# First mixer of a two-block transformer in fp32: gates and output projections with tokens on the partitions, and an earlier start condition for the differential heads

## What is computed

```python
h = rmsnorm(x, norm_mix_g)
u = h @ w_in                                   # 1024 x 5376
u_rwkv, u_attn, u_gate = split(u, [1792, 3328])
o_a = rwkv7_time_mix(u_rwkv, ...)              # 256 x 512
o_b = diff_attention(u_attn, ...)              # 256 x 512, 4 heads
g_a, g_b = split(sigmoid(u_gate), 2)           # 256 x 1024 each
merged = g_a * (o_a @ w_proj_a) + g_b * (o_b @ w_proj_b)
x = x + merged @ w_out
h = rmsnorm(x, norm_mlp_g)                     # and on to w_ff1, w_ff2, ...
```

## Time and profile before

| | us |
|---|---|
| median of 3 runs | 1442.97 (1442.38 to 1443.07) |
| time of the profiled execution | 1442.83 |
| span of the profiled execution | 1441.0 |
| TensorE busy (matmuls) | 1431.8 |
| VectorE busy | 1015.3 |
| ScalarE busy | 766.0 |

### The profile page before, as it was taken

One profiled execution on the slowest core, in us unless ns is written; L12 is line 12 of the kernel. 1 busy time (PEld: TensorE's weight loads), 2 busy tenths in 40 slices (PEclk: granted clock), 3 DMA queues, 4 the chain that ended last, 5 costly groups with the idle time before them and its releaser, 6 DMA issues.

```text
span 1441.0 us, 22851 instructions
## 1 busy us (share of the span) xinstructions
PE 1431.8 (99%) x9408; PEld 1233.0 (86%) x9408; DVE 1015.3 (70%) x1347; ACT 766.0 (53%) x1038; POOL 26.3 (2%) x93
## 2 busy tenths in 40 slices
PE   9999999999999999999999999999999999999999
PEld 8988898888888888888878888888888877788887
DVE  6866577886457887558768786478774688688753
ACT  7744474655336555445766555355553556665532
POOL 0000000000001100000000000000000000000000
PEclk9999999999999999999999999999999999999999
DMA  8431225555554555545424555545555453255552
GB/s 335 172 121 62 89 102 220 197 204 189 191 175 176 205 186 194 194 157 205 147 90 174 198 183 201 183 171 205 178 202 185 160 181 135 91 204 186 194 188 86
DMA packets 36103, 249.11 MB, mean 173 GB/s; under 512 B 4128, under 2 KB 4256, under 8 KB 6688
## 3 DMA queue, kind: packets, MB, share of 16 engines
q1 hardware_dynamic: 35712, 247.46, 48.3%
q10 hardware_dynamic: 288, 0.19, 0.1%
HBM read 246.59 MB, written 1.05 MB: 172 GB/s over the span
## 4 chain that ended last, share of the span: by engine, by line
PE 97%; DMA 1%; ACT 1%; DVE 1%; issue 0%; SPq 0%; DVEq 0%; ACTq 0%
PE ps L2007 24%; PE ps L1922 16%; PE ps L1924 16%; PE ps L1923 16%; PE ps L2014 12%; PE ps L1997 2%; PE ps L2143 1%; PE ps L1996 1%; DMA raw<-ws 1%; PE ps L2064 1%; PE ps L2340 1%; PE ps L2320 1%; PE ps L2173 1%; PE ps L2329 0%; PE ps L1993 0%; ACT hi L2371 0%
## 5 line engine op out<-in xcount | busy, mean ns | idle before, releaser
L2693 DVE TENSOR_TENSOR lo<-raw,hi 128x2048 fp32r<-128x2048 f32 (+1 forms) x230 | 525.3, 2285 | 221.6 <-ACT hi L2371 221.3
L2371 ACT CAST hi<-raw 128x2048 fp32r<-128x2048 f32 (+1 forms) x230 | 438.0, 1905 | 246.1 <-PE ps L1924 242.3
L2007 PE MATMUL ps<-h,hi 128*128 128x512 f32 x1504 | 359.1, 390 | 0.0
L2007 PEld LDWEIGHTS ps<-h,hi 128*128 128x128 f32 x1504 | 276.4, 188 | 52.3
L1922 PE MATMUL ps<-hi,a 128*128 128x512 f32 x584 | 230.1, 394 | 0.0
L1924 PE MATMUL ps<-hi,a 128*128 128x512 f32 x584 | 227.6, 390 | 0.0
L1923 PE MATMUL ps<-lo,a 128*128 128x512 f32 x584 | 227.4, 389 | 0.0
L2014 PEld LDWEIGHTS ps<-h,lo 128*128 128x128 f32 x1504 | 192.2, 190 | 7.9
L2014 PE MATMUL ps<-h,lo 128*128 128x256 f32 x1504 | 194.4, 282 | 0.0
L2556 ACT COPY a<-ps 128x256 f32<-128x256 f32 x208 | 76.6, 372 | 206.4 <-PE ps L2007 102.8
L1922 PEld LDWEIGHTS ps<-hi,a 128*128 128x128 f32 x584 | 109.7, 188 | 23.9 <-issue 2.0
(11 more groups left out here) (347 smaller groups left out, 1556.6 us busy)
## 6 DMA issues: line engine op xcount, KB each, us to landing
raw<-ws SPq DMA_DIRECT2D x229, 1024.0 KB, 4.8
X<-xin SPq DMA_DIRECT2D x8, 256.0 KB, 5.3
raw<-ws SPq DMA_DIRECT2D x2, 512.0 KB, 6.6
out<-X SPq DMA_DIRECT2D x4, 256.0 KB, 2.1
small<-small SPq DMA_DIRECT2D x1, 992.5 KB, 12.8
const<-const SPq DMA_DIRECT2D x1, 900.0 KB, 6.6
a<-row SPq DMA_DIRECT2D x1, 512.0 KB, 7.8
const<-const SPq DMA_DIRECT2D x1, 388.0 KB, 13.2
```

What stands on the lines that cost most here:

```text
L2007: t = e.matmul(b2(s["slots"][u]), wh[:, k, 128 * u:128 * u + 128], h2[:, k, :, :], start=k == 0, stop=last)
L2371: e.copy(hi[j % NSPL][:, n], raw[j % NRAW][:, n]).then_inc(hi_ready, 1)
L2693: e.tensor_tensor(lo[j % NSPL][:, n], raw[j % NRAW][:, n], hi[j % NSPL][:, n].bitcast(F), ALU.subtract).then_inc(lo_ready, 1)
```

## The change

1. The 2048 gate columns are cut into pieces of 4 k-tiles by 512 columns and done in kind `rows`; `gA` and `gB` have tokens on the partitions, and the evacuation (`gate_in`) multiplies by the tokens' rstd as a per-partition scalar.
2. `w_proj_b` and `w_proj_a` are done in kind `rows` too (their pieces hold the same data); `pb` and `pa` work on a bank of 128 tokens by 512 features, and `pa` ends after the addition of `gB`.
3. The gated sum is turned: a new step `m_turn`, four transposes on TensorE, then ScalarE's cast from the bank to `mH` and VectorE's subtraction from the bank to `mL`. There are four of them, for half 0 or 1 of the features and b = 0, 1: (0,0) after the first half of `w_proj_a`, (0,1) four filler steps into the second half, (1,0) after it, (1,1) four steps into `w_out`. `x_again` waits for the last one.
4. `diff` begins once `bonus` has been read, not `("bk", 1)`.

```diff
     deep("w_in", 0, 8, 2816, 512)
-    cols("w_in", 0, 8, 3328, 2048, 256)
+    for c in range(3328, 5376, 512):
+        deep("w_in", 0, 8, c, 512)
...
-        gB = Arena(0)([128, 8, S])
+        gB = Arena(0)([128, 2, D])
...
-        gA = X[:, :, :].rearrange("p b (n s) -> p (b n) s", s=S)
+        gA = X
...
         def diff():
-            while "vd" not in state or ("bk", 1) not in state:
+            while "vd" not in state or "bonus" not in state:
...
+            def gate_in(g, half):
+                def evac(sl, b, h):
+                    emit("gate_in", dve=0.7, slot=sl, g=g, b=b, half=half, rstd=nm.rstd)
+                    state["g" + g, half] = sl
+                return evac
+
+            for g, c in (("A", 3328), ("B", 4352)):
+                for half in range(2):
+                    yield from rows_mat("w_in", 0, 8, c + 512 * half, 512, "h", nm.h_needs, gate_in(g, half))
...
+        def m_turn(half, b):
+            sl = take()
+            emit("m_turn", slot=sl, b=b, half=half, v=merged[half, b], v_hi=merge_a.add())
+            give(sl)
+            m_at[half, b] = (free[sl.b], sl.n)
...
+        straight(rows_mat("w_proj_a", 0, 4, 0, 512, "oa", oa_needs, pa(0)))
+        m_turn(0, 0)
+        spread(rows_mat("w_proj_a", 0, 4, 512, 512, "oa", oa_needs, pa(1)), [lambda: m_turn(0, 1)], 4)
+        m_turn(1, 0)
...
+        def last_turn():
+            m_turn(1, 1)
+            emit("x_again", last=m_at[1, 1])
+
+        spread(rows_into_x("w_out", 0, 8, "m", lambda k, b: m_at[k // 4, b], x_add((1.0, 1.0)), nm), [last_turn], 4)
...
+                elif kind == "m_turn":
+                    claim(sl)
+                    e.wait_ge(merge_v.sem, s["v"])
+                    for u in range(4):
+                        c = 512 * s["half"] + 128 * u
+                        t = e.transpose(banks[sl.b][:, 128 * u:128 * u + 128], gA[:, s["b"], c:c + 128], ident)
                     t.then_inc(full[sl.b], 1)
...
+                elif kind == "m_turn":
+                    b, k = s["b"], 4 * s["half"]
+                    ready(sl)
+                    e.copy(mH[:, k:k + 4, 128 * b:128 * b + 128], b4(sl)).then_inc(merge_a.sem, 1)
...
+                elif kind == "gate_in":
+                    b, o = s["b"], slice(512 * s["half"], 512 * s["half"] + 512)
+                    e.wait_ge(rstd_ready.sem, s["rstd"])
                     ready(sl)
+                    e.tensor_scalar({"A": gA, "B": gB}[s["g"]][:, b, o], banks[sl.b][:, :], rstd[b], None,
+                                    ALU.mult).then_inc(free[sl.b], 1)
...
                 elif kind == "pa":
...
-                    e.tensor_tensor(g, b2(sl), g, ALU.mult).then_inc(free[sl.b], 1)
+                    e.tensor_tensor(gA[:, b, o], banks[sl.b][:, :], gA[:, b, o], ALU.mult).then_inc(free[sl.b], 1)
                     read_out(sl)
-                    e.tensor_tensor(g, g, gB[:, n:n + 2, :], ALU.add).then_inc(merge_v.sem, 1)
+                    e.tensor_tensor(gA[:, b, o], gA[:, b, o], gB[:, b, o], ALU.add).then_inc(merge_v.sem, 1)
+                elif kind == "m_turn":
+                    b, k = s["b"], 4 * s["half"]
+                    out_ = slice(128 * b, 128 * b + 128)
                     e.wait_ge(merge_a.sem, s["v_hi"])
-                    e.tensor_tensor(mL[:, n:n + 2, :], g, mH[:, n:n + 2, :].bitcast(F), ALU.subtract).then_inc(merge_v.sem, 1)
+                    e.tensor_tensor(mL[:, k:k + 4, out_], b4(sl), mH[:, k:k + 4, out_].bitcast(F),
+                                    ALU.subtract).then_inc(free[sl.b], 1)
```

More of the change, by code:

```diff
@@ L1569, in mixers_fill, with pb, evac @@
                 yield None
[L1571 to L1577, removed]
+            def pb(half):
+                def evac(sl, b, h):
+                    emit("pb", dve=0.7, slot=sl, b=b, half=half, sig=state["sig", "B", half])
+                return evac
+            for half in range(2):
+                if half:
                     yield "pe"
@@ L1581, in mixers_fill @@
                         yield None
-                yield from cols_piece("w_proj_b", 0, c, "ob", lambda k: (diff_v.sem, state["ob_v"]), pb)
+                yield from rows_mat("w_proj_b", 0, 4, 512 * half, 512, "ob", lambda k, b: (diff_v.sem, state["ob_v"]),
+                                    pb(half))
         weave([shifts(), rwkv_decays(), rwkv_keys(), (rwkv_chain(), LEAD), (rwkv_block(0), LEAD), (rwkv_block(1), LEAD),
@@ L1586, in program, with pa, evac, oa_needs @@
               [mixers_fill(nm)])
[L1588 to L1596, removed]
+        m_at = {}
+        merged = {}
+        def pa(half):
+            def evac(sl, b, h):
+                emit("pa", slot=sl, b=b, half=half, sig=state["sig", "A", half], v=merge_v.add())
+                merged[half, b] = merge_v.n
+            return evac
+        def m_turn(half, b):
[3 more added lines that the diff above has]
+            m_at[half, b] = (free[sl.b], sl.n)
+        def oa_needs(k, b):
+            return (rwkv_v.sem, max(rwkv_v.at["oal0"], rwkv_v.at["oal1"]))
+        straight(rows_mat("w_proj_a", 0, 4, 0, 512, "oa", oa_needs, pa(0)))
+        m_turn(0, 0)
+        spread(rows_mat("w_proj_a", 0, 4, 512, 512, "oa", oa_needs, pa(1)), [lambda: m_turn(0, 1)], 4)
+        m_turn(1, 0)
         for b in range(2):
@@ L1600, in program @@
         nm = Norm("norm_mlp_g", table=False)
-        straight(rows_into_x("w_out", 0, 8, "m", lambda k, b: (merge_v.sem, 2 * (k // 2) + 2), x_add((1.0, 1.0)), nm))
+        def last_turn():
+            m_turn(1, 1)
+            emit("x_again", last=m_at[1, 1])
+        spread(rows_into_x("w_out", 0, 8, "m", lambda k, b: m_at[k // 4, b], x_add((1.0, 1.0)), nm), [last_turn], 4)
         emit("tail_in", x=xt[0, 0])
@@ L2064, in tensor_program @@
                         t = e.transpose(banks[sl.b][:, 128 * u:128 * u + 128], X[:, s["b"], c:c + 128], ident)
+                    t.then_inc(full[sl.b], 1)
+                elif kind == "m_turn":
[4 more added lines that the diff above has]
+                        t = e.transpose(banks[sl.b][:, 128 * u:128 * u + 128], gA[:, s["b"], c:c + 128], ident)
                     t.then_inc(full[sl.b], 1)
@@ L2540, in scalar_program @@
                 elif kind == "gate_sig":
-                    part = {"A": gA, "B": gB}[s["g"]][:, 4 * s["half"]:4 * s["half"] + 4, :]
+                    part = {"A": gA, "B": gB}[s["g"]][:, :, 512 * s["half"]:512 * s["half"] + 512]
                     if s["table"]:
@@ L2998, in vector_program @@
                 elif kind == "pb":
-                    n = s["n"]
+                    b, o = s["b"], slice(512 * s["half"], 512 * s["half"] + 512)
                     e.wait_ge(gate_a.sem, s["sig"])
                     ready(sl)
-                    e.tensor_tensor(gB[:, n:n + 2, :], b2(sl), gB[:, n:n + 2, :], ALU.mult).then_inc(free[sl.b], 1)
+                    e.tensor_tensor(gB[:, b, o], banks[sl.b][:, :], gB[:, b, o], ALU.mult).then_inc(free[sl.b], 1)
                     read_out(sl)
@@ L3004, in vector_program @@
                 elif kind == "pa":
-                    n = s["n"]
-                    g = gA[:, n:n + 2, :]
+                    b, o = s["b"], slice(512 * s["half"], 512 * s["half"] + 512)
                     e.wait_ge(gate_a.sem, s["sig"])
                     ready(sl)
-                    e.tensor_tensor(g, b2(sl), g, ALU.mult).then_inc(free[sl.b], 1)
+                    e.tensor_tensor(gA[:, b, o], banks[sl.b][:, :], gA[:, b, o], ALU.mult).then_inc(free[sl.b], 1)
                     read_out(sl)
-                    e.tensor_tensor(g, g, gB[:, n:n + 2, :], ALU.add).then_inc(merge_v.sem, 1)
+                    e.tensor_tensor(gA[:, b, o], gA[:, b, o], gB[:, b, o], ALU.add).then_inc(merge_v.sem, 1)
+                elif kind == "m_turn":
+                    b, k = s["b"], 4 * s["half"]
+                    out_ = slice(128 * b, 128 * b + 128)
@@ L3264, in sync_program @@
                 elif kind == "x_again":
-                    e.wait_ge(merge_v.sem, s["v"])
+                    e.wait_ge(s["last"][0], s["last"][1])
                     for b in range(2):
```

13 lines of the change are left out of this document (1 added, 12 removed).

## The result

| | before | after |
|---|---|---|
| median (12 runs each) | 1442.77 | 1446.36 |
| time of the profiled execution | 1442.83 | 1446.13 |
| span of the profiled execution | 1441.0 | 1444.3 |

The ratio is 1.0023, 95% interval 1.0016 to 1.0031: the change makes the kernel 3.6 us slower. The forecast of 1442.6 is missed, and so is its range of 1440.6 to 1445.6. Eight of the 12 runs of after have a mean granted clock of 0.998 or 0.999 and times of 1446.13 to 1446.94, four have 1.000 and 1444.89 to 1445.38, and the profiled execution is one of the eight.

A forecast was written before the change was run, and what follows sets the result against it. TensorE's steps were taken to bound the kernel (busy 1431.8 of 1441.0 us). Terms -2.40 - 0.78 + 1.80 + 0.9 - 0.2 + 0.3 = -0.38 us gave 1442.6 against the median, no change, range 1440.6 to 1445.6.

The forecast's parts named there:

- The RWKV output (loss): At `w_proj_a`, TensorE asks for `oa` before it is ready at 215.30: +0.3 us, within 0 to 0.84.
- Rival 1: Slower: the heads' early start delays the RWKV chain and TensorE stands still; 1448.1 us with the whole shift; chance 0.16.
- Earlier heads: In the weave, heads start about 5 us earlier, which only covers a 1 us wait at `w_proj_b`; set at zero.
- Gates: In the gate pieces, 192 long matmuls at 0.2275 us replace 384 short ones at 0.1200: -2.40 us.
- Projections: In the output projections, 96 long matmuls at 0.2275 us replace 192 short ones at 0.1178: -0.78 us.
- Turns: Four groups of four transposes between TensorE's long matmuls, 0.45 us each: +1.80 us.
- The turns' waits: TensorE waits at the first turn for `pa` on VectorE, later turns have more room: +0.9 us, 0.1 to 1.4.
- Residual's load: `x_again` on SP's queue goes out 3 us earlier, ending a wait at the first norm turn: -0.2 us.
- Rival 2: Long matmuls bring no gain in gates and projections: +2.8 us, 1445.8; chance 0.03.
- Rival 3: Faster: no turn waits, `oa` comes in time, and the weave needs fewer returns to filler: 1440.4 us; chance 0.12.

The follow-up runs named there:

- e2: The kernel before (columns layout) with only the heads' early start added; 1441.63 us.
- e6: The kernel after with one planner number changed, three long matmuls costed at 3 x 0.24 us in place of 3 x 0.227; 1441.45 us.
- e9: e2 with one planner number changed, two groups of short matmuls costed at 2 x 0.345 us in place of 2 x 0.36; 1447.89 us.
- e4: The kernel after with 12 idle matmuls of 512 columns into a spare bank ahead of `w_proj_a`; 1445.42 us.
- e1: The kernel after with the heads' old start condition put back; 1453.63 us.
- e10: e6 with the output projections fed from the normed input in place of `oa` and `ob`; 1441.41 us, one run.
- e8: e6 with each of the four turns' transposes issued twice, 32 in place of 16; 1443.27 us.
- e5: The kernel after with the RWKV tail ordered by hand on ScalarE and VectorE, other sigmoids and weight splits later; 1444.86 us.
- e3: The kernel after with the gates' sigmoids held back until `oa` is planned; 1447.28 us.

## Why the prediction was wrong

Three stretches of TensorE, from the first matmul of V to the first of `w_proj_b`, from there to the first of `w_out`, and on to the first norm turn (L2064 before, L2077 after):

| us | V to `w_proj_b` | to `w_out` | to norm turn | sum |
|---|---|---|---|---|
| before | 123.69 | 22.62 | 16.55 | 162.86 |
| after | 120.86 | 28.92 | 16.95 | 166.73 |
| e2 | 122.54 | 22.62 | 16.42 | 161.58 |
| e6 | 120.73 | 24.33 | 16.90 | 161.96 |

What follows the norm turn takes 1195.6 to 1195.9 us in all four. The 3.9 us between the sums of before and after are the 3.3 us between the spans, the first matmul of V having come 0.35 us earlier in the profile after, and 0.2 us at the end.

- **The step that failed is "The RWKV output (loss)", +0.3 us within 0 to 0.84.** TensorE's request was forecast for 214.46 and came at 214.04. `oa` was left at 215.30 "if nothing else moves", and came at 216.8. It moved because the planner makes a new order for the whole weave from the costs of the new steps: the last sums were issued at 201.95 in place of 200.02, behind the gates and no longer in front of 5 us of them. TensorE went on 2.9 us after its request. e6 and e9 show it from both sides: the same instructions in another order give 4.9 us back in one layout and cost 6.3 us in the other.
- **A wait has a second price.** The forecast reckoned waits one for one. Behind 2.7 us of standing the trace shows 1.5 us lost at the low clock, and e4's trace gets them back. Wait and clock, 2.9 + 1.5 = 4.4 us by the trace, are more than the whole loss.
- **Rival 1 named the right place and condition and the wrong cause.** Its point ("no filler is left and TensorE stands still") was met, but taking the heads' early start back is no cure: without it the kernel is 7.3 us slower (e1), and with it the sums can stand 5 us earlier than in before (e6). Of the 1.9 us by which the last sums came late, e1 leaves 1.2 open to rival 1. The heads also moved by more than the 5 us of the forecast: they begin at 103.1 in place of 110.33, 7 us earlier, and `ob` is ready at 189.5 in place of 204.36, 15 us earlier.
- **"Earlier heads: zero" was too low.** In the columns layout they give 1.1 us (e2). The wait that they save in the rows layout was put at 1 us and is 7.2 in e1.
- **Gates, -2.40 forecast.** The first stretch is 1.7 us shorter from e2 to after and 1.8 to e6. The long matmuls of the gates came 0.2275 to 0.231 apart, not 0.2275 throughout. Over all neighbours with nothing between them the mean is 0.2299 us in the kernel after and 0.1195 for the short ones before: 384 x 0.1195 - 192 x 0.2299 = 45.89 - 44.14 = 1.75, which is what the stretch shows. The four rounds of the earlier trace rows were a short sample. By the rule of the Trainium skill that the forecast set beside it ("TensorE: Matmul & The Clock Gate", section "Back-to-back issue gap") they would have gained an estimated 0.5 us; the traces do not agree, in either layout (0.1195 and 0.2299 us where the rule has 0.109 and 0.216).
- **Projections, -0.78 forecast, -0.2 measured.** They came 0.2333 apart: 96 x 0.2333 = 22.4 us against 22.6. The first matmuls of `w_out` ran at 0.229 to 0.231. e10 puts 0.4 us of it on the operand. The row for this term was V's, with another operand, and no row of before showed `oa` or `ob` as stationary.
- **Turns, +1.80 forecast, right.** 0.44 us each by the trace, 0.455 by e8, and the transposes between full-rate matmuls left the clock at 1.00.
- **The turns' waits, +0.9 forecast.** The first turn did not wait in the kernel after, since `w_proj_a` itself had waited; the third did, 0.5 us. In e6, without the big wait, it is 0.3 us at the first. The range of 0.1 to 1.4 holds it, the value was too high.
- **Residual's load, -0.2 forecast, right.** The matmul behind the first norm turn comes 0.59 us after the one ahead of it in e6, 0.80 in before.
- **The sum by what was measured:** gates -1.7, projections -0.2, turns +1.8, their waits +0.5, the load -0.2, the RWKV output with the clock +4.4, the heads -1.1 (from the columns layout) make +3.5 us, against 3.3 between the spans and 3.6 between the medians.
- **Rival 2** (no gain from long matmuls) is nearly true of the projections and false of the gates. **Rival 3** gave 1440.4 for a weave that closes up; the best order found stops at 1441.45.

With a good order the change comes to, by the table, e6 against e2: gates -1.8, all that follows +2.2 (the turns 1.8 of it), so +0.4 us, and by the medians to nothing (1441.45 and 1441.63). The layout is a draw. The 3.6 us that the change costs, and 1.3 more, went when its steps were put in another order.

Not settled: why exactly the planner's order tips. It is known only that a cost of 0.681 us for three long matmuls leaves none of the gates' matmuls behind the last sums, and one of 0.72 leaves 33.

## What to carry to other kernels

Where a planner orders the work from costs written by hand, a change of tile shape is also a change of order: look for what is left beside the last dependent chain (here 5.0, 0 and 7.6 us of filler behind the same sums) before adding up instructions. Shortening the filler that covers a chain is only a gain while the chain ends before it. Price a wait of TensorE above its length (here by up to 1.5 us), and try the planner's numbers before any hand-made order: one number gave 4.9 us where two orders by hand gave -0.9 and 1.5.

## What was not expected of the hardware

- After TensorE had stood for 2.7 us its granted clock was 0.50 in the window 218 to 220, with full work in it; behind the standstills of 2.0 (e5), 2.4 (e9) and 3.6 us (e3) the lowest windows have 0.54, 0.52 and 0.50; behind those of 0.3, 0.5 and 1.7 us (the last in e9) the rows stay at 1.00.
- The fall did not come in every run: four of the 12 of after have a mean clock of 1.000, and their median is 1.6 us under that of the other eight, about the 1.5 us that the trace puts on the slow matmuls. That the wait was as long in these four is likely and not shown, since only one execution was traced.
- The same matmul of 128x512 is issued every 0.2267, 0.2275 to 0.231 or 0.2333 us in neighbouring stretches at a granted clock of 1.00. The change of operand in e10 moved it from 0.2331 to 0.2269 at the start of the projections.
